# Two compression blocks of decode from three products instead of four, in a two-layer inference step

## The reference, cut to what matters

```python
def compress_rows(rows, pos_emb, w1, w2):
    B, L = rows.shape[:2]
    nc = (L - CMP_BLOCK) // CMP_STRIDE + 1
    idx = jnp.arange(nc)[:, None] * CMP_STRIDE + jnp.arange(CMP_BLOCK)[None, :]
    blk = rows[:, idx] + pos_emb[None, None, :, None, :]
    blk = jnp.swapaxes(blk, 2, 3).reshape(B, nc, NSA_KV_HEADS, CMP_BLOCK * HEAD_DIM)
    return jax.nn.gelu(blk @ w1) @ w2
```

## Time and profile before

| | |
|---|---|
| median of 3 runs (lowest to highest) | 1865.57 us (1865.45 to 1867.22) |
| the profiled execution | 1868.04 us |
| its span, first to last instruction | 1866.3 us |
| mean granted clock of TensorE | 0.998 of full speed |
| TensorE busy | 1838.7 us, 99% |
| VectorE, ScalarE, GpSimd busy | 1204.6, 372.3, 119.1 us |
| chain that ended last, on TensorE | 94% |

### The profile page before, as it was taken

How to read it: one execution, slowest core, us unless ns; L and a number is a source line. 1 busy time by engine, 2 the same in 40 slices (tenths; PEclk the granted TensorE clock), 3 DMA queues, 4 the chain that set the end, 5 groups by cost and what they waited for, 6 DMA issues and landing times.

```text
span 1866.3 us, 27349 instructions
## 1 busy us (share of the span) xinstructions
PE 1838.7 (99%) x10438; PEld 1412.1 (76%) x10438; DVE 1204.6 (65%) x2676; ACT 372.3 (20%) x957; POOL 119.1 (6%) x218
## 2 busy tenths in 40 slices
PE   8999999999999999999999999999999999999999
PEld 7767777877777777777777676777777777777777
DVE  5899796442667677673268997954427667676631
ACT  2013375322100100000001134842211000100000
POOL 1011400110000000000000114001000000000000
PEclk9999999999999999999999999999999999999999
DMA  7302564663112222131242044057431212222111
GB/s 276 129 1 88 161 209 157 214 221 111 57 68 72 87 68 90 58 136 63 80 152 79 1 122 143 1 182 249 161 122 45 90 69 80 78 70 109 72 62 51
DMA packets 110390, 199.86 MB, mean 107 GB/s; under 512 B 13393, under 2 KB 81250, under 8 KB 105266
## 3 DMA queue, kind: packets, MB, share of 16 engines
q1 hardware_dynamic: 90946, 161.87, 25.5%
q0 software_dynamic: 5488, 29.93, 4.6%
q10 hardware_dynamic: 13824, 6.30, 1.3%
HBM read 190.36 MB, written 15.94 MB: 111 GB/s over the span
## 4 chain that ended last, share of the span: by engine, by line
PE 94%; DVE 4%; ACT 1%; issue 1%; DMA 0%; POOL 0%; DVEq 0%
PE ps L1065 30%; PE ps L1130 15%; PE ps L755 12%; PE ps L616 8%; PE ps L651 8%; PE ps L603 7%; PE ps L859 2%; PE ps L822 2%; PE ps L841 2%; PE ps L999 1%; PE ps L659 1%; PE ps L893 1%; PE ps L908 1%; PE ps L695 1%; PE ps L862 1%
## 5 line engine op out<-in xcount | busy, mean ns | idle before, releaser
L2140 DVE TENSOR_TENSOR xT<-xT,ps 128x288 f32<-128x288 f32 (+3 forms) x55 | 41.7, 758 | 153.2 <-PE ps L1130 152.9
L1065 PE MATMUL ps<-catT,rD 128*128 128x288 f32 x528 | 131.6, 406 | 0.0
L1065 PEld LDWEIGHTS ps<-catT,rD 128*128 128x128 f32 x528 | 100.3, 190 | 27.7
L1497 ACT ACTIVATE rD<-rD 128x592 f32<-128x592 f32 x44 | 30.7, 697 | 450.2 <-DVE rD L2082 450.2
L755 PE MATMUL ps<-WR,rD 128*128 128x254 f32 (+1 forms) x512 | 120.2, 382 | 0.2
L1065 PE MATMUL ps<-catT,XC 128*128 128x288 f32 x480 | 119.8, 406 | 0.4 <-DVE rD L2054 0.4
L1065 PE MATMUL ps<-rA,WR 128*128 128x288 f32 x448 | 117.8, 406 | 0.0
L1065 PEld LDWEIGHTS ps<-catT,XC 128*128 128x128 f32 x480 | 91.0, 190 | 26.2 <-issue 1.2
L755 PEld LDWEIGHTS ps<-WR,rD 128*128 128x128 f32 x512 | 93.0, 188 | 18.6 <-issue 2.9
L1065 PEld LDWEIGHTS ps<-rA,WR 128*128 128x128 f32 x448 | 85.1, 190 | 23.5
L616 PE MATMUL ps<-catT,WR 128*128 128x288 f32 x384 | 98.8, 410 | 2.0 <-ACT catT L1231 1.1
(11 more groups left out here) (376 smaller groups left out, 3317.7 us busy)
## 6 DMA issues: line engine op xcount, KB each, us to landing
WR<-in_w_up SPq DMA_DIRECT2D x56, 512.0 KB, 3.7
WR<-in_kvc SPq DMA_DIRECT2D x128, 128.0 KB, 2.3
rB<-in_w_up SPq DMA_DIRECT2D x32, 512.0 KB, 4.3
rD<-in_kvc SPq DMA_DIRECT2D x96, 128.0 KB
rD<-in_w_down SPq DMA_DIRECT2D x8, 1408.0 KB, 7.6
rB<-in_ksT SPq DMA_DIRECT2D x160, 64.0 KB, 4.0
rB<-in_w_down SPq DMA_DIRECT2D x6, 1408.0 KB, 6.0
WR<-in_w_glu SPq DMA_DIRECT2D x16, 512.0 KB, 3.9
```

The source lines that it names most:

```text
L1065: ins = mm(ps[:, bank, 0:HN], w[:, k, :], h[:, k, :], start=k == 0, stop=k == 3)
L2140: step(tt(x, x, src, ALU.add))
```

## The change: three products, and sums of chunks and of weights

Two blocks, c = 2m and 2m + 1, are made together. With the even chunks E(m) = x(2m) and the odd ones O(m) = x(2m + 1), the three products are B E, A O and (A + B)(E + O). The even block is the third minus the other two; the odd block 2m + 1 is A O(m) + B E(m + 1). Each product has 8 weight tiles and 128 columns (64 pairs by 2 heads): `third(i, part)`, part 0, 1 and 2, written side by side in the half's bank. A + B is made once in a layer (`weight_sums_of`), in the space of the convolution's history, of `YB` and of the causal mask, which are free then; history and mask are loaded again behind the pairs. E + O is made in place in the cache rows (`row_sums`), for each half, on VectorE. ScalarE copies the three results out of PSUM (`thirds_kept`), and `gelu_in_joined` puts them together. Only the nine halves in `decode` are changed. In pairs 0 to 2 the order on TensorE is now: a wait for `cmp_max`; thirds (0, 0), (0, 1), (1, 0), (0, 2); the probabilities and the importance as before; (1, 1), (1, 2), (2, 0), then half of (2, 1), or in pair 2 all of (2, 1) and (2, 2); the rest of half 2 where it was before. The wait for `cmp_max` stands ahead of pair 3's filling products as well. The core of the diff:

```diff
         w1 = [rD[:, 4096 + 2048 * i:6144 + 2048 * i].rearrange("p (j m) -> p j m", j=16) for i in range(2)]
+        kept = [rC[:, 8568:8824], rA[:, 4432:4560]]
+        wab = [[XC[:, c, XS0 + P * i:XS0 + P * (i + 1)] for c in range(CT) for i in range(2)],
+               [t[:, P * i:P * (i + 1)] for t in (YB, causal) for i in range(4)]]
         sq2 = [rD[:, 576 * i:576 * (i + 1)] for i in range(2)]
...
-                sp.wait_ge(*count("conv_made", CT))
-                sp.wait_ge(*count("uc_out", 16))
-                if l + 1 < DEPTH:
-                    sp.dma_start(XC[:, :, XS0:XW], I["hist"][l + 1].rearrange("p (c n) -> p c n", c=CT)).then_inc(sh["hist_in"], 16)
...
+                if l + 1 < DEPTH:
+                    sp.wait_ge(sh["hid_made"], 16 * (l + 1))
+                    sp.dma_start(XC[:, :, XS0:XW], I["hist"][l + 1].rearrange("p (c n) -> p c n", c=CT)).then_inc(sh["hist_in"], 16)
+                    sp.dma_start(causal[:, :], I["c_causal"]).then_inc(sh["causal_in"], 16)
...
-                    def half(i, js=range(16)):
+                    def third(i, part, js=range(NPAIR)):
+
                         job, b, n, c, bank = HALVES[p][i]
-                        earlier = [h for h in late if h[0] * 2 + h[2] < job * 2 + n and h[4] == bank]
-                        hidden(l, job, b, n, js=js, bank=bank, taken=2 * earlier[-1][0] + earlier[-1][2] + 1 if earlier else 6)
+                        if part == 0 and js[0] == 0:
+                            if n == 0:
+                                pe.wait_ge(*count(f"kv_in{rows_at(b)}", 256))
+                            if i == 2:
+                                pe.wait_ge(sh["hb_kept"], 9 * l + 3 * p + 1)
+                            elif p:
+                                pe.wait_ge(sh["hb_kept"], 9 * l + 3 * p - (0 if i == 0 else 1))
+                            elif i == 0:
+                                pe.wait_ge(sh["cmp_in"], 16 * l + 7)
+                        if part == 2 and js[0] == 0:
+                            pe.wait_ge(sh["hs_made"], 9 * l + 3 * p + i + 1)
+                            if p == 0:
+                                pe.wait_ge(sh["ab_made"], 2 * l + 2 - n)
+                        rows = kvc[rows_at(b)][:, 0:32 * PAST // CHUNK].rearrange("p (m q e) -> p q m e", q=2, e=32)[:, 1 if part == 1 else 0]
+                        for j in js:
+                            o = n * 16 + j * 2
+                            w = (w1[n][:, NPAIR + j, :], w1[n][:, j, :], wab[n][j])[part]
+                            ins = mm(thirds(bank)[part], w, rows[:, :, o:o + 2], start=j == 0, stop=j == NPAIR - 1)
+                        if js[-1] == NPAIR - 1 and part != 1:
+                            ins.then_inc(sh["hid_made" if part else "hb_made"], 1)
...
+                    pe.wait_ge(*count("cmp_max"))
                     if more:
-                        half(0)
+                        third(0, 0)
+                        third(0, 1)
+                        third(1, 0)
+                        third(0, 2)
...
                     if more:
-                        half(1)
-                        half(2, range(9) if p < 2 else range(16))
+                        third(1, 1)
+                        third(1, 2)
+                        third(2, 0)
+                        if p < 2:
+                            third(2, 1, range(4))
+                        else:
+                            third(2, 1)
+                            third(2, 2)
...
-                            half(2, range(9, 11))
+                            third(2, 1, range(4, 8))
...
-                            pe.wait_ge(sh["cmp_in"], 16 * (l + 1))
+                            pe.wait_ge(sh["hb_kept"], 9 * (l + 1))
...
                         if j == 5 and p < 2:
-                            half(2, range(11, 12))
+                            third(2, 2, range(1))
...
                             if p < 2:
-                                half(2, range(12, 14))
+                                third(2, 2, range(1, 3))
...
                             if p < 2:
-                                half(2, range(14, 15))
+                                third(2, 2, range(3, 5))
...
                         if p < 2:
-                            half(2, range(15, 16))
+                            third(2, 2, range(5, 8))
...
+                    def thirds_kept(i):
+                        act.wait_ge(sh["hid_made"], 16 * l + 8 + 3 * p + i)
+                        if 3 * p + i:
+                            act.wait_ge(sh["hx_made"], 9 * l + 3 * p + i)
+                        bank = HALVES[p][i][4]
+                        copy(kept[0], ps[:, bank, 0:2 * P])
+                        copy(kept[1], ps[:, bank, 2 * P:3 * P]).then_inc(sh["hb_kept"], 1)
...
                     if more:
-                        fetch_keys(range(8))
+                        fetch_keys(range(7))
...
                     if more:
-                        tanhed(tanh[0], NCS)
-                        fetch_keys(range(8, 16))
+                        thirds_kept(0)
+                        fetch_keys(range(7, 13))
                     act.wait_ge(*count("s_masked"))
                     act.activation(S[:, 0:2056], S[:, 0:2056], ACT.Exp, bias=st[:, 14:15], scale=SCALE, accum_out=st[:, 16:17]).then_inc(sh["s_exped"], 1)
                     if more:
+                        tanhed(tanh[0], NCS)
+                        thirds_kept(1)
                         tanhed(tanh[1], NCS)
                         if p == 2:
+                            thirds_kept(2)
                             tanhed(tanh[2], NCS)
...
+                        fetch_keys(range(13, 16))
                         keys_kept(NCS, KcT[ba % 4])
...
                     if p < 2:
+                        thirds_kept(2)
                         tanhed(tanh[2], NCS)
...
+            def row_sums(b, n):
+
+                dve.wait_ge(*count("hb_made"))
+                rows = kvc[rows_at(b)][:, 0:32 * PAST // CHUNK].rearrange("p (m q e) -> p q m e", q=2, e=32)[:, :, :, 16 * n:16 * (n + 1)]
+                tt(rows[:, 0], rows[:, 0], rows[:, 1], ALU.add).then_inc(sh["hs_made"], 1)
+
+            def gelu_in_joined(n, s, bank):
+
+                dve.wait_ge(*count("hb_kept"))
+                count("hid_made")
+                first, second, third = [t.rearrange("p (m h) -> p m h", h=2) for t in (kept[0][:, 0:P], kept[0][:, P:2 * P], kept[1])]
+                even, odd = each_other(CX[s][n], 0, 64), each_other(CX[s][n], 1, 63)
+                step(tt(even, first, second, ALU.add))
+                stt(odd, second[:, 0:63], posb[:, n:n + 1], first[:, 1:64], ALU.add, ALU.add)
+                stt(even, third, posb[:, n:n + 1], even, ALU.add, ALU.subtract).then_inc(sh["hx_made"], 1)
+                dve.wait_ge(*count("hx_made"))
+                x, g = CX[s][n][:, 0:2 * NCS], CG[s][n][:, 0:2 * NCS]
+                step(stt(g, x, 0.044715, x, ALU.mult, ALU.mult))
+                stt(g, g, 1.0, x, ALU.add, ALU.mult).then_inc(sh["cmp_in"], 1)
+
+            def weight_sums_of(n):
+                if n:
+                    for t, i in ((YB, 0), (causal, 4)):
+                        ins = tt(t.rearrange("p (j m) -> p j m", j=4), w1[1][:, i:i + 4], w1[1][:, NPAIR + i:NPAIR + i + 4], ALU.add)
+                else:
+                    ins = tt(XC[:, :, XS0:XS0 + 2 * P].rearrange("p c (i m) -> p c i m", i=2),
+                             w1[0][:, 0:NPAIR].rearrange("p (c i) m -> p c i m", i=2),
+                             w1[0][:, NPAIR:2 * NPAIR].rearrange("p (c i) m -> p c i m", i=2), ALU.add)
+                ins.then_inc(sh["ab_made"], 1)
...
+                if l:
+                    dve.wait_ge(sh["causal_in"], 16 * l)
...
+                weight_sums_of(1)
+                dve.wait_ge(sh["uc_out"], 16 * (l + 1))
+                weight_sums_of(0)
...
+                    halves_of = [(n, c, bank) for job, b, n, c, bank in HALVES[p]]
+                    rows_of = [(b, n) for job, b, n, c, bank in HALVES[p]]
+                    if more:
+                        row_sums(*rows_of[0])
...
                     if more:
-                        gelu_in(*halves_of[0], banks_of[0])
+                        row_sums(*rows_of[1])
...
                     if more:
-                        gelu_out(*halves_of[0])
-                        gelu_in(*halves_of[1], banks_of[1])
+                        gelu_in_joined(*halves_of[0])
+                        row_sums(*rows_of[2])
+                        gelu_out(halves_of[0][0], NCS, halves_of[0][1])
+                        gelu_in_joined(*halves_of[1])
                         if p == 2:
-                            gelu_in(*halves_of[2], banks_of[2])
-                        gelu_out(*halves_of[1])
+                            gelu_in_joined(*halves_of[2])
+                        gelu_out(halves_of[1][0], NCS, halves_of[1][1])
                         if p == 2:
```

(13 more changed lines are left out.)

1 line of the change is left out of this document (removed).

## The result

The changed kernel takes 1875.17 us (median of ten runs, 1871.50 to 1877.94), the kernel before 1866.53 beside it (ten runs, 1865.45 to 1868.71): ratio 1.0043, 95% interval 1.0033 to 1.0053. It is slower by 8.6 us, and 1.2 us above the upper end of the forecast range. The profiled execution took 1877.28 us, of which 1875.5 are span. Its mean granted clock is 0.991; before, it was 0.998. The ten runs lie in two groups: four from 1871.5 to 1872.3, at a clock of 0.995, and six from 1874.9 to 1877.9, at 0.991 to 0.994.

What follows compares the result with a forecast made beforehand. First guess: TensorE, 99% busy, is the bound; its saved 29 us go to waits. Pairs -0.75, +0.1, -0.05, +0.7 make 0.0 a layer; handshakes add +0.8 to 1865.57: 1866.4 us, range 1857 to 1874.

Steps and rivals of the forecast that it cites:

- the fall of the clock: Rival: stalls in decode drop TensorE to 1.2 GHz, four times 1.65, +6.6, 1873 us; chance 0.11.
- the rule of the Trainium skill that the prediction cited against itself: TensorE: waits between bursts of products halve the clock again, so each stall would be paid for a second time.
- Pace of the narrow records: Decode's 128-column products on TensorE: 0.113 us a record, so a half goes from 7.04 to 5.42.
- Pause: TensorE idle before the first third, waiting for `cmp_max`: 1.7 us in pair 0, 2.5 in pairs 1 and 2.
- VectorE one microsecond late: Pairs 1 and 2: L1901 on VectorE starts 1.03 us late behind the previous pair's last third, and `cmp_max` with it.
- Stages without clock: Start to importance +2.8 (pairs 1, 2), +0.7 (pair 3); importance to weighting -2.1, pair 2 -2.85; weighting to next pair -0.6.
- Pair 0: Start to importance product in pair 0: 1.66 us of waiting plus 0.3 for four products, +1.95.
- The +0.4 a layer for handshakes: More handshakes between engines, uncounted waits of 0.03 to 0.14 us, some five on the path: +0.8 in two layers.
- The profile's signs: Decode afterwards: 0.113 a record, TensorE idle before first thirds, exp 0.3 us sooner, probability copies 10.5 (pair 2: 13.3) behind L954.
- three signs of being wrong: In decode: joined form not near 1.7 us, granted clock under 1.00, L1901 not a microsecond late.
- Price of a fall: Each fall of TensorE's clock in decode costs 1.65 us; four of them, +6.6.
- Row sums hidden: VectorE's `row_sums`, 1.22 us each, run beside other products ahead of the importance product and were called hidden there.

Runs made afterwards that it cites:

- e3_before_with_wait: The kernel before, with only the wait for `cmp_max` added ahead of half 0 and of pair 3's filling products: 1876.53 us, ratio 1.0056.
- e9_tail_moved: The changed kernel with the last half's gelu input and output of pairs 0 and 1 moved into the next pair, behind `pc_ready`: 1868.50 us, ratio 1.0011.
- e12_change_again: The changed kernel itself, unedited, measured once more: 1875.43 us, ratio 1.0041 to the kernel before.
- e4_no_row_sums: The changed kernel with `row_sums` adding one pair of chunks instead of 64: 1870.38 us, ratio 1.0024 to the kernel before.
- e7_wait_behind_one: The changed kernel with the `cmp_max` wait behind third (0, 0) in pairs 0 and 1: 1867.72 us, ratio 0.9999 to the kernel before.
- e8_before_long_pause: The kernel before, with TensorE's wait for `pc_ready` moved ahead of half 0 in pairs 0 to 2: 1891.46 us, ratio 1.0138.
- e1_filled_stall: The changed kernel with dummy products of ones ahead of the `cmp_max` wait in pairs 0 to 2: 1869.53 us, ratio 1.0013 to the kernel before.
- e2_wait_moved: The changed kernel with the `cmp_max` wait behind thirds (0, 0) and (0, 1), dropped in pair 3: 1865.60 us, ratio 0.9991 to the kernel before.

## Why the prediction was wrong

The step that failed stands among the rivals: "A stall of 2.5 us behind the small products in pairs 1 and 2 is shorter than that." From that, the fall of the clock got a chance of 0.11, and the sum had nothing for it. It fell behind all four of these pauses, in both profiles of the changed kernel. I compared the pause with the 4 us of the earlier trace rows, of which TensorE had worked 1.5; that is one example of a fall, and says nothing of what shorter pauses do. It was also the wrong length to compare: the pause in that row is the 1.70 us at 233.32, and the 2.5 us expected in decode are longer. Over the profiles above, pauses of 1.3 to 1.5 us ahead of the first product of a pair (e3_before_with_wait, e9_tail_moved, and pair 0 of the change, of e12_change_again and of e4_no_row_sums) were followed by a slow stretch in 0 of 18 cases, pauses of 2.4 to 2.6 in 16 of 20 (the change, e4_no_row_sums, e7_wait_behind_one, e8_before_long_pause and e12_change_again). The trace agrees with the rule of the Trainium skill that the prediction cited against itself (TensorE: Matmul & The Clock Gate, HAM oscillation): waits between bursts were paid for twice, in 16 of these 20 cases. The section's own example has longer waits than these, and waits for loads.

Point by point:

- Pace of the narrow records: 0.113 forecast, 0.112 the median start to start. Right; 128 columns stand on the floor of the weights.
- Pause: 2.48 forecast in pairs 1 and 2, 2.37 measured beyond the small products. VectorE one microsecond late: L1988 starts 3.85 behind the pair's start (344.35 - 340.50), L1901 before 2.76: 1.09 late, 1.03 forecast. Right, and it matters: the kernel before pauses 1.30 with the same wait and keeps its clock, and e9_tail_moved takes that microsecond away and keeps it too. The order of two VectorE blocks decides.
- Stages without clock: +2.66 for +2.8, +0.65 for +0.7, -2.14 for -2.1, -2.92 for -2.85, -0.62 for -0.6. Right.
- Pair 0: +1.95 forecast, +0.63 measured. A term mis-sized by 1.3: its row was not clean. The small products of pair 0 before took 4.07 us with gaps of "issue", against 2.98 in pair 1 and in e3_before_with_wait. So 1.1 of the 11.80 us that I added to are such gaps, which the profile after has not, and the pause was 1.44 instead of the 1.66 that I read the earlier trace rows. Against a clean 10.70, as in pair 1, the 12.43 measured are +1.73. The +0.4 a layer for handshakes was not there either. Without the clock, decode is at -3.3 instead of +0.8: 2.5 us of that are pair 0 of the two layers, 0.8 the handshakes.
- The profile's signs: the joined form takes 1.85 us (341.67 to 343.52) for 1.72, the exp starts 5.15 behind L987 in pair 0 for the 5.14 forecast, and the copies of the turned probabilities 10.48 and 13.24 (pair 2) behind it for 10.5 and 13.3. Right. Of the three signs of being wrong one came, the granted clock under 1.00.
- Price of a fall: 1.65 forecast, 1.44 and 1.66 measured; but I counted four, and there were also two at pair ends and two more than before in the prompt parts, together 5.4 us. That is why the time lies outside the range although the rival's own sum, 1873, is near.
- Row sums hidden: 0.24 a pair by e4_no_row_sums, 1.4 us in all, so not quite. Weight sums and the loads moved: no wait for them in the trace after.

What is shown and what is not: e1_filled_stall and e8_before_long_pause show that the pause drops the clock, in the change and without it. The slow stretches at pair ends and in the prompt parts came and went from run to run in several kernels, and nothing here was made to test them; the second one in the prompt parts stood also in profiles of e2_wait_moved, e3_before_with_wait and e9_tail_moved. One count speaks for the change at the pair ends: from the first weighted sum to the next pair, the eleven profiles of kernels with three products have a slow stretch in 18 of 66 cases, the three with four products (before, e3_before_with_wait, e8_before_long_pause) in 0 of 18. The former have waits of some 1.1 us ahead of `keys_second`, which the latter lack. Of the 9.2 us between the two profiled executions, decode's starts are 6.2; that the other stretches belong to the change is not shown. Why four of twenty pauses of 2.4 to 2.6 us, one of the longest among them, passed without a fall is open.

## What to carry to other kernels

Before a full engine's filler is made shorter or gated, price every pause twice: its length, and a slow stretch behind it (1.4 to 1.7 us here, behind most pauses of 2.4 us and none of 1.3). Give a wait the place of its first real reader: two thirds ahead of it brought the time back to that of the kernel before (ratio 0.9991), though not below it. Then look for what was in time only because the kernel was slower: here a load that nobody had waited for came next, and cost 6 to 8 us in one pair of each layer. An engine that gets ahead also starts other transfers sooner (here the gathers, by 8 us), and they can fall on the load that is now late. Only with pair 2 reordered and the window loads held back was it a gain, of 5 to 8 us. And read a term from two places of a trace; a row with gaps of "issue" in it put 1.3 us too many into one of mine.

## What the runs showed that I had not expected

- Useless products sped the kernel up: 20 records of ones in a pause made the next 48 useful ones 1.44 us shorter.
- Of two kernels one wait of SyncE apart, one was 0.3 to 0.4% faster than before (two measurements) and one 0.1% slower: the wait delayed the issue of sequence 6's rows by 4.65 us and brought them beside the gathered loads.
- 16 loads of 128 KB landed within some 2.3 us in the median over the whole kernel, but in e2_wait_moved up to 8.1 us behind their issues (8.6 in layer 1) where the gathered loads ran beside them; the DMA share from 370 to 376 is 0.99 there. I suspected the window loads and held those back; the gathers I did not try.
- Gaps of "issue" in the small products of pair 0, 1.1 and 0.9 us in the two layers, stand in four of the fourteen profiles: in that of before, and in the three that were taken where the kernel before took 1868.27 instead of 1865.8 to 1866.0. The other ten have none. That they make that difference of 2.4 us is likely and not shown.
